# One pool of eight PSUM banks in both mixers, the bank chosen by the step that lets it go

## The chip, the cores and the metric

The kernel runs on one core of a Trainium2 chip. The time is the device time of one execution in microseconds (us), the median of several. The core's engines work beside one another and meet at semaphores: TensorE (PE) multiplies matrices into PSUM, VectorE (DVE) and ScalarE (ACT) read and write PSUM and SBUF, GpSimd (POOL) works on SBUF, SyncE (SP) issues the weight DMAs. PSUM has eight banks of 128 partitions x 512 fp32 values.

## The reference, cut to what matters

A batch of one sequence, 512 tokens of 1024 features, goes through seven parts in a row. The change touches the first and the sixth.

```python
h = x
h = h + mamba2_mixer(rmsnorm(h, ...), ...)                 # first mixer
h = h + swiglu_ffn(rmsnorm(h, ...), ...)                   # ffn 0
h = h + conformer_conv_module(rmsnorm(h, ...), ...)
h = h + swiglu_ffn(rmsnorm(h, ...), ...)                   # ffn 1
x = rmsnorm(h, final_norm)                                 # first block ends
x = x + 0.5 * g1 * swiglu(modulate(rmsnorm_2(x, ...), ...), ...)   # ffn 2
x = x + g2 * (merged @ w_out)     # second mixer: window attention (8 heads, sink) and
                                  # differential attention (4 heads), RoPE, gated and merged
x = x + 0.5 * g3 * swiglu(modulate(rmsnorm_2(x, ...), ...), ...)   # ffn 3
```

The first mixer is a Mamba-2 layer: one projection gives z (16 tiles of 128 features), x (16 tiles), B and C (4 groups each) and the step sizes dt; x, B and C go through a causal convolution of 4 taps and silu; then the state-space scan in 4 chunks of 128 tokens for 32 heads, a norm per group with the gate z, and the output projection.

## The kernel before

Activations lie transposed: h is 8 tiles of 128 features x 512 tokens. A linear layer is a helper (`linear`, L477): for each of its input tiles three matmuls of 128x128 weights on 512 tokens (L486 to L488), since operand and weight are each split in a rounded part (XH, WH) and a rest (XL, WL). Weights come in one long stream of 391 chunks of 8 tiles: SP loads a chunk into `raw`, ACT or POOL rounds it, POOL makes the rest.

Every engine runs its own program, written as a plain sequence. In the mixers all programs go through the same list of steps, `mamba_order()` (L99) and `mixer_order()` (L127), each doing its share of a step. A step of the first mixer is "u", "b", "c" (a tile of x, B, C), "z", "o" (an output tile of the group before), "dec", "A" (the products "cb" of C and B, and B transposed into "Bt"), "B", "C", "D" (transposes "xt" of x, the states "st" in the three banks "S", the first two heads "p"), "E" (two heads' output "Y" and the next two "p"), "H" and "I" (the group's sum of squares "gq" and its spread "qw"). In the second mixer "sA", "vA", "pA" are scores, transposes and products of the window attention, "sB", "tB", "pB" those of the differential one, "k1" to "q2" norm and rotation ("tf", "tw", "rot"), "l" a linear (q, k, v, the gates ga and gb, the branch ba).

Whatever PE makes is a block with a key and needs a PSUM bank. `bank(key, of)` (L456) takes the next one of the tuple `of` in turn and, if an earlier block holds it, waits for the mark ("free", holder), which DVE or ACT sets with the instruction that reads the holder last. A wait stops everything behind it in PE's sequence. `linear` asks for the banks of all its keys before its first matmul. The turn is kept in a dictionary whose key is the tuple itself.

- First mixer: LIN = (0, 1, 2) for linears, TR = (3, 4) for transposes, heads, "cb", "dec", "gq", "qw", SY = (5, 6, 7) for the states and Y; its first linears, eight blocks in all, use ALL (L499).
- Second mixer: MIX = (0, 1, 2, 3, 4), SB = (5, 6) for "sB", OB = (7,) for the window attention's output (L782); its last two loops of linears, "bb" and "wo", use ALL.
- Feed-forward parts: ALL, all eight in turn. Conformer: CB = (0, 1, 2, 3, 4) and XB = (5, 6, 7) (L722); its first linear takes two pairs of banks from CB and XB.

The whole program is built twice: the first pass counts each engine's marks, the second one knows for every key which count of which semaphore it is (`Steps.known`).

Of the kernel before, what the change touches and what calls it, by code (L numbers as in the profile page):

```python
# [175 lines left out]

class Steps:
# [3 lines left out]
    def __init__(self, known=None):  # L181
        self.known, self.made, self.sems = known, {}, {}
# [17 lines left out]
class Counter:  # L200
# [25 lines left out]
def build(nc, dram, steps):  # L226
    at, noted = steps.at, steps.noted
    stream = []
    with ExitStack() as ctx:
# [221 lines left out]
        def pe_program(e):  # L451
            w = Waits(e)
            did = steps.counter("pe")
            turn, holds = {}, {}

            def bank(key, of):  # L456

                n = turn[of] = turn.get(of, -1) + 1
                b = of[n % len(of)]
# [17 lines left out]
            def linear(keys, tiles, slots, ready, of, between=None):  # L477

                bs = [bank(k, o) for k, o in zip(keys, of if isinstance(of[0], tuple) else [of] * len(keys))]
# [17 lines left out]
            ALL, LIN, TR, SY, LO = tuple(range(8)), (0, 1, 2), (3, 4), (5, 6, 7), (0, 1, 2, 3)  # L497
# [38 lines left out]
            def mamba():  # L536
# [7 lines left out]
                def factor(i):  # L544

                    if i == NT - 2:
                        w.wait_ge(s_cst, 16)
                        sum_of("s0", ALL)
                    if i == NT - 1:
                        w.wait_ge(*at("rstd", "s0"))  # L550
                        spread(("s0", "w"), small("s0"), ALL)

                linear([("dt", 0), ("u", 16), ("u", 20), ("u", 0)], [dts, tile(16), tile(20), tile(0)], X8, raw_x, ALL,
                       factor)
                linear([("u", 1)], [tile(1)], X8, raw_x, ALL)
                linear([("u", 2)], [tile(2)], X8, raw_x, ALL)
# [19 lines left out]
                for what, g, i in mamba_order():  # L576
                    par = g % 2
                    if what in ("u", "b", "c"):
                        m = conv_tile((what, g, i))
                        if m not in FIRST:  # L580
                            linear([("u", m)], [tile(m)], X8, raw_x, LIN)
                    elif what == "z":
                        linear([("z", 4 * g + i)], [column("ssm_w_in", 0, 4 * g + i)], X8, raw_x, LIN)
                    elif what == "o":
                        linear([("o", g, i)], [[wt("ssm_w_out", 0, 4 * g + j, i) for j in range(4)]],
                               [8 + 4 * par + j for j in range(4)], lambda j: ("x", "g", 4 * g + j), LIN)
                    elif what == "dec":
                        b = bank(("dec", 0), TR)
# [5 lines left out]
                        b = bank(("dec", 1), TR)  # L594
                        w.wait_ge(*at("dg"))
                        e.matmul(b[:, 0:P], ones, dt_dg, start=True, stop=True).then_inc(*did(("sum", "dec", 1)))
                    elif what == "A":
                        b = bank(("cb", g), TR)
# [6 lines left out]
                        turned(("Bt", g), Bf[par], 3, TR)  # L605
                    elif what in "BCD":
                        if what == "C":
                            S = [bank(("S", g, c), SY) for c in range(3)]
# [3 lines left out]
                        if what in "BC":  # L612
                            for j in ((0, 1) if what == "B" else (2, 3)):
                                w.wait_ge(*at("uv", 4 * g + j))
                                turned(("xt", g, j), xs[par][j], 4, TR)
# [3 lines left out]
                    elif what == "E":  # L619
                        n = 8 * g + 2 * i  # L620
                        Y = bank(("Y", g, i), SY)
# [1590 lines left out]
```

## Time and profile before

| | us |
|---|---|
| median of 3 runs | 2612.82 (2610.52 to 2614.27) |
| the profiled execution | 2610.64 |
| its span, first to last instruction | 2608.8 |
| PE / DVE / POOL / ACT busy | 2516.2 / 1265.1 / 1048.6 / 920.8 |
| mean granted TensorE clock | 0.976 |

The granted clock is 1.00 at 2.4 GHz and 0.5 at 1.2 GHz; a stretch of 0.75 was half the time at either. Durations in a timeline are those of one instruction (or of a merged group, then with its count) on one engine; matmuls overlap, so one of 512 columns has 0.39 us of its own, while 24 in a row take 5.44 us. A bracket behind a row is the time that the engine was idle before it, with the engine and line of the instruction that released it. The line can be a helper's: L1406 is the helper for a scalar-tensor-tensor instruction, L533 that of the transposes, L502 the token sums. In the tiles' names the numbers of buffers are left out: `arena` holds most tiles of the mixers.

### The profile page before, as it was taken

Reading aid. Unit: us, or ns where it says so; the run is one execution under the profiler, and the core shown is the slowest. Engines: PE = TensorE matmul, PEld = TensorE weight load, DVE = VectorE, ACT = ScalarE, POOL = GpSimd, SP = SyncE. Lnnn points to the kernel's source line nnn. Section 1 sums busy time; section 2 is a strip of 40 time slices with the busy share of each in tenths; the row PEclk is TensorE's granted clock in tenths of the full one; section 3 lists DMA queues with packets and bytes.
Section 4 is the critical chain, followed back from the end, with each engine's and each line's share of the span. In section 5 each row is a group of like instructions: output and inputs, shape, how many; then the busy total and the mean of one; then the engine's idle time right before and its main releaser. Section 6 shows DMA issues by size and latency. Waiting matters only on the chain.

```text
span 2608.8 us, 29205 instructions
## 1 busy us (share of the span) xinstructions
PE 2516.2 (96%) x11835; PEld 2054.5 (79%) x11835; DVE 1265.1 (48%) x2010; ACT 920.8 (35%) x1527; POOL 1048.6 (40%) x480
## 2 busy tenths in 40 slices
PE   8989998899999999999999999999999999999999
PEld 6768887788888887788888788887766678788887
DVE  6766666554445697454434632225355545422222
ACT  3424434222223386222223232223455553222221
POOL 4333343544444410654444444443322234544442
PEclk9989999899999998999999999999999999999999
DMA  4112221354442310354432233332211112223222
GB/s 152 49 49 68 70 75 57 126 179 162 161 161 96 98 33 9 129 180 161 162 113 96 90 97 97 97 97 73 73 49 49 49 58 96 81 97 97 97 97 89
DMA packets 70982, 252.56 MB, mean 97 GB/s; under 512 B 8000, under 2 KB 8512, under 8 KB 70848
## 3 DMA queue, kind: packets, MB, share of 16 engines
q1 hardware_dynamic: 58752, 210.27, 25.0%
q10 hardware_dynamic: 12096, 40.42, 4.3%
q8 instruction: 94, 1.54, 0.2%
q14 instruction: 40, 0.33, 0.0%
HBM read 248.56 MB, written 2.10 MB: 96 GB/s over the span
## 4 chain that ended last, share of the span: by engine, by line
PE 85%; DVE 10%; ACT 4%; issue 1%; POOL 0%; ACTq 0%; DMA 0%; DVEq 0%; POOLq 0%
PE ps L486 25%; PE ps L487 25%; PE ps L488 25%; PE ps L502 2%; DVE tmpm L1406 1%; DVE arena L1406 1%; PE ps L526 1%; DVE XL L1415 1%; PE ps L564 1%; PE ps L533 1%; PE ps L717 1%; PE ps L719 1%; PE ps L718 1%; PE ps L632 1%; PE ps L863 1%
## 5 line engine op out<-in xcount | busy, mean ns | idle before, releaser
L2103 POOL TENSOR_TENSOR WL<-raw,WH 128x1024 fp32r<-128x1024 f32 x391 | 951.0, 2434 | 1277.6 <-ACT WH L902 1270.8
L486 PE MATMUL ps<-XH,WH 128*128 128x512 f32 x3160 | 1253.0, 397 | 35.4 <-DVE XL L1406 15.5
L487 PE MATMUL ps<-XL,WH 128*128 128x512 f32 x3160 | 1239.1, 392 | 0.0
L488 PE MATMUL ps<-XH,WL 128*128 128x512 f32 x3160 | 1238.6, 392 | 0.0
L486 PEld LDWEIGHTS ps<-XH,WH 128*128 128x128 f32 x3160 | 600.5, 190 | 170.9 <-issue 22.8
L488 PEld LDWEIGHTS ps<-XH,WL 128*128 128x128 f32 x3160 | 598.8, 190 | 126.6
L487 PEld LDWEIGHTS ps<-XL,WH 128*128 128x128 f32 x3160 | 600.4, 190 | 124.4 <-issue 2.2
L902 ACT ACTIVATE WH<-raw 128x1024 fp32r<-128x1024 f32 x306 | 322.3, 1057 | 738.6 <-PE ps L488 603.6
L1406 DVE SCALAR_TENSOR_TENSOR arena<-arena,ps 128x512 f32<-128x512 f32 x88 | 60.4, 686 | 525.2 <-ACT arena L1098 512.4
L2101 POOL CAST WH<-raw 128x1024 fp32r<-128x1024 f32 x85 | 98.2, 1156 | 261.0 <-PE ps L488 239.2
L1406 DVE SCALAR_TENSOR_TENSOR h<-ps,der,h 128x512 f32<-128x512 f32 x104 | 77.4, 750 | 160.4 <-PE ps L488 160.2
L1456 DVE TENSOR_TENSOR h<-h,ps 128x512 f32<-128x512 f32 x128 | 85.4, 684 | 93.3 <-PE ps L488 92.9
L1102 ACT ACTIVATE XH<-ps 128x512 fp32r<-128x512 f32 x88 | 52.7, 599 | 177.5 <-DVE ps L1720 92.2
L1415 DVE TENSOR_TENSOR XL<-ps,XH 128x512 fp32r<-128x512 f32 x92 | 63.5, 690 | 58.6 <-ACT XH L1102 58.5
L1682 DVE CUSTOM_DVE_ANT_0 arena<-arena 128x1024 f32<-128x1024 f32 x72 | 91.9, 1313 | 0.0
L1098 ACT ACTIVATE arena<-ps 128x512 f32<-128x512 f32 x88 | 51.6, 587 | 65.0 <-DVE ps L1712 49.5
L1406 DVE SCALAR_TENSOR_TENSOR arena<-ps,vec,arena 128x512 f32<-128x512 f32 (+29 forms) x95 | 64.6, 726 | 0.4
L1406 DVE SCALAR_TENSOR_TENSOR tmpm<-ps,der,tmpm 128x509 f32<-128x509 f32 (+2 forms) x72 | 53.9, 749 | 21.4 <-ACT tmpm L979 19.7
L1712 DVE TENSOR_TENSOR ps<-ps,rsm 128x512 f32<-128x512 f32 x44 | 30.5, 694 | 38.6 <-PE ps L488 34.0
L919 ACT ACTIVATE tmpm<-h 128x512 f32<-128x512 f32 x49 | 30.5, 623 | 52.0 <-DVE h L1406 41.6
L1406 DVE SCALAR_TENSOR_TENSOR XL<-h,vec,XH 128x512 fp32r<-128x512 f32 x32 | 36.4, 1138 | 24.2 <-ACT XH L911 24.2
L998 ACT ACTIVATE arena<-ps,arena 128x128 f32<-128x128 f32 x128 | 36.4, 370 | 21.4 <-PE ps L564 21.4
(250 smaller groups left out, 1935.0 us busy)
## 6 DMA issues: line engine op xcount, KB each, us to landing
raw<-in_w SPq DMA_DIRECT2D x394, 512.0 KB, 3.7
arena<-in_w_mod ACTq DMA_DIRECT2D x72, 512.0 KB, 4.4
o_out<-h SPq DMA_DIRECT2D x8, 256.0 KB, 2.0
h<-in_x SPq DMA_DIRECT2D x4, 256.0 KB, 7.2
h<-in_x ACTq DMA_DIRECT2D x4, 256.0 KB, 6.4
raw<-in_w SPq DMA_DIRECT2D x2, 256.0 KB, 4.1
arena<-in_c ACTq DMA_DIRECT2D x1, 512.0 KB, 6.3
vec<-in_vec ACTq DMA_DIRECT2D x1, 295.5 KB, 9.8
```

The lines of the kernel that those rows point to most:

```text
L486: e.matmul(b, wh, XH[:, x, :], start=i == 0, stop=False)
L487: e.matmul(b, wh, XL[:, x, :], start=False, stop=False)
L488: p = e.matmul(b, wl, XH[:, x, :], start=False, stop=i == len(slots) - 1)
L502: p = e.matmul(b[:, c * n:(c + 1) * n], src[:, c * P:(c + 1) * P], mat, start=start and c == 0, stop=stop and c == 3)
L902: A(WH[:, c % NSPL, :], raw[:, c % NRAW, :], ACT.Copy).then_inc(*did(("hi", c)))
L1102: A(XH[:, 8 + 4 * (g % 2) + i, :], ps("up", n, j), ACT.Copy).then_inc(*did(("xhi", "a", n, j)))
L1406: return e.scalar_tensor_tensor(out=out, in0=a, scalar=s, in1=b, op0=op0, op1=op1)
L1415: TT(XL[:, slot, :], src, XH[:, slot, :].bitcast(F32), SUB).then_inc(*did(("x", *key), *free))
L1456: TT(h[:, m, :], h[:, m, :], ps(*key), ADD).then_inc(*marks)
L1682: e.tensor_tensor_reduce(out=t, in0=t, in1=crow, scale=1.0, scalar=0.0, op0=MUL, op1=ADD, accum_out=modv[:, i:i + 1]).then_inc(*did(("mod" ...
L2101: e.tensor_copy(hi, x).then_inc(*did(("hi", c)))
L2103: e.tensor_tensor(lo, x, hi.bitcast(F32), SUB).then_inc(*did(("split", c)))
```

## The change

Both mixers' blocks (all that had ALL, LIN, TR, SY or (5,) in the first, ALL, MIX, SB or OB in the second, up to "bb") take their bank from one pool of eight, named ANY. In the second pass of the build the bank is the one whose holder is let go at the earliest (stage, step), where the stage is the part (0 to 6) and the step the place in the mixer's list at which the engine that sets ("free", holder) does so; a bank without holder, and all that is let go outside a list, counts as (stage, 0) or lower, and ties go by turn. In the first pass the pool goes by turn. ACT's and DVE's programs note stage and step as they go; their instructions, their order and those of PE stay as they are.

```diff
+def placed(stage, order):
+
+    return (((stage, k + 1), step) for k, step in enumerate(order))
...
     def __init__(self, known=None):
-        self.known, self.made, self.sems = known, {}, {}
+        self.known, self.made, self.sems, self.now = known, {}, {}, (0, 0)
...
             self.steps.made[k] = (self.name, self.n)
+            if k[0] == "free":
+                self.steps.note(("let go", *k[1:]), self.steps.now)
...
             turn, holds = {}, {}
+            ANY = None
+
+            def let_go(b):
+
+                n = (b - turn[ANY] - 1) % 8
+                return (*(steps.known["let go", *holds[b]] if b in holds else (0, 0)), n)
 
             def bank(key, of):
 
-                n = turn[of] = turn.get(of, -1) + 1
-                b = of[n % len(of)]
+                if of is ANY and steps.known:
+                    turn.setdefault(of, -1)
+                    b = turn[of] = min(ALL, key=let_go)
+                else:
+                    n = turn[of] = turn.get(of, -1) + 1
+                    b = (of or ALL)[n % len(of or ALL)]
                 if b in holds:
                     w.wait_ge(*at("free", *holds[b]))
...
-            ALL, LIN, TR, SY, LO = tuple(range(8)), (0, 1, 2), (3, 4), (5, 6, 7), (0, 1, 2, 3)
+            ALL = tuple(range(8))
...
-                linear([("u", 3)], [tile(3)], X8, raw_x, (5,))
+                linear([("u", 3)], [tile(3)], X8, raw_x, ANY)
...
-                    b = bank(("p", n), TR)
+                    b = bank(("p", n), ANY)
...
-                            S = [bank(("S", g, c), SY) for c in range(3)]
+                            S = [bank(("S", g, c), ANY) for c in range(3)]
...
-                MIX, SB, OB = (0, 1, 2, 3, 4), (5, 6), (7,)
...
-                            b = bank(("sB", hd, qb, t), SB)
+                            b = bank(("sB", hd, qb, t), ANY)
...
-                for what, g, i in mamba_order():
+                for steps.now, (what, g, i) in placed(0, mamba_order()):
...
-                for what, n, i in mixer_order():
+                for steps.now, (what, n, i) in placed(5, mixer_order()):
...
-            mamba()
-            ffn(0)
-            conformer()
-            ffn(1)
-            ffn(2)
-            mixer()
-            ffn(3)
+            for stage, (does, *n) in enumerate(((mamba,), (ffn, 0), (conformer,), (ffn, 1), (ffn, 2), (mixer,), (ffn, 3))):
+                steps.now = stage, 0
+                does(*n)
```

The last three pieces stand in ACT's and DVE's programs. All other requests of the two mixers change from their tuple to ANY in the same way.

## Rows read from the trace of the kernel before

**Rows 1.** From the page: busy time and share of each engine, and the chain that ended last.

```profile
PE 2516.2 (96%) x11835; PEld 2054.5 (79%) x11835; DVE 1265.1 (48%) x2010; ACT 920.8 (35%) x1527; POOL 1048.6 (40%) x480
...
PE 85%; DVE 10%; ACT 4%; issue 1%; POOL 0%; ACTq 0%; DMA 0%; DVEq 0%; POOLq 0%
```

**Rows 2.** Timeline of PE, first mixer: start, duration, group xcount [idle before <-releaser].

```profile
61.67 2.07 PE L603 MATMUL ps<-arena 128*128 128x128 f32 x8 [4.76 <-DVE arena L1406]
...
83.11 2.93 PE L572 MATMUL ps<-arena 128*128 128x128 f32 x12 [4.60 <-DVE arena L1406]
...
146.91 1.86 PE L502 MATMUL ps<-cst,summ 128*128 128x1 f32 x8 [4.77 <-DVE arena L1613]
...
167.87 1.11 PE L533 MATMUL ps<-cst,arena 128*128 128x128 f32 x4 [4.75 <-DVE arena L1406]
...
245.97 1.05 PE L502 MATMUL ps<-cst,summ 128*128 128x1 f32 x8 [1.97 <-DVE arena L1613]
...
268.43 0.50 PE L486 MATMUL ps<-XH,WH 128*128 128x512 f32 x1 [1.28 <-DVE arena L1406]
...
467.26 0.79 PE L486 MATMUL ps<-XH,WH 128*128 128x512 f32 x1 [2.42 <-DVE h L1456]
...
477.38 0.77 PE L486 MATMUL ps<-XH,WH 128*128 128x512 f32 x1 [5.70 <-DVE h L1456]
```

**Rows 3.** Timeline of PE, second mixer.

```profile
1846.75 0.50 PE L486 MATMUL ps<-XH,WH 128*128 128x512 f32 x1 [0.93 <-ACT tmpm L1292]
...
1875.44 1.12 PE L814 MATMUL ps<-arena 128*128 128x512 f32 x2 [0.82 <-ACT tmpm L1292]
...
1936.28 1.65 PE L825 MATMUL ps<-arena 64*128 64x384 f32 x2 [5.08 <-DVE arena L1995]
...
1999.84 1.01 PE L825 MATMUL ps<-arena 64*128 64x384 f32 x2 [3.15 <-DVE arena L1406]
...
2015.62 0.91 PE L825 MATMUL ps<-arena 64*128 64x384 f32 x2 [1.46 <-DVE arena L1995]
```

**Rows 4.** Table by stretch: length, busy time (xcount) of the five engines, granted clock, DMA share, GB/s.

```profile
40.61:46.05 5.44, 5.44 (x25) 4.51 (x25) 4.49 (x9) 0.60 (x1) 3.44 (x2) 1.00 0.29 93
148.79:156.33 7.54, 7.54 (x26) 6.06 (x27) 0.18 (x1) 0.26 (x1) 0.00 (x0) 0.73 0.00 0
169.00:176.58 7.58, 7.58 (x26) 6.02 (x26) 3.81 (x7) 0.60 (x1) 0.00 (x0) 0.71 0.05 21
347.33:357.54 10.21, 8.26 (x33) 6.82 (x34) 2.08 (x4) 3.59 (x5) 1.85 (x2) 0.83 0.16 52
464.86:484.59 19.73, 11.62 (x37) 9.11 (x38) 10.69 (x12) 7.32 (x10) 4.73 (x3) 0.74 0.42 131
2014.17:2024.22 10.05, 8.60 (x32) 6.46 (x34) 5.61 (x18) 3.40 (x8) 1.30 (x2) 0.83 0.17 53
```

**Rows 5.** Timeline of DVE, first mixer.

```profile
63.77 0.69 DVE L1613 TENSOR_TENSOR arena<-ps,cst 128x512 f32<-128x512 f32 x1 [1.44 <-PE ps L603]
...
82.36 0.69 DVE L1406 SCALAR_TENSOR_TENSOR arena<-ps,tmpm 128x512 f32<-128x512 f32 x1
...
93.42 0.69 DVE L1604 TENSOR_TENSOR arena<-ps,rsm 128x512 f32<-128x512 f32 x1 [4.02 <-PE ps L488]
...
172.99 0.56 DVE L1570 TENSOR_TENSOR arena<-arena 128x384 f32<-128x384 f32 x1
...
184.29 0.69 DVE L1604 TENSOR_TENSOR arena<-ps,rsm 128x512 f32<-128x512 f32 x1 [2.47 <-PE ps L488]
...
469.27 0.68 DVE L1456 TENSOR_TENSOR h<-h,ps 128x512 f32<-128x512 f32 x1
```

**Rows 6.** Timeline of PE, then of DVE, where the conformer part begins.

```profile
843.15 0.39 PE L486 MATMUL ps<-XH,WH 128*128 128x512 f32 x1
...
846.42 0.67 DVE L1456 TENSOR_TENSOR h<-h,ps 128x512 f32<-128x512 f32 x1
```

**Rows 7.** Timeline of DVE, second mixer.

```profile
2014.87 0.69 DVE L1995 TENSOR_TENSOR arena<-ps,arena 128x512 f32<-128x512 f32 x1
```

More of the change, by code:

```diff
@@ L477, in linear @@
             def linear(keys, tiles, slots, ready, of, between=None):
-                bs = [bank(k, o) for k, o in zip(keys, of if isinstance(of[0], tuple) else [of] * len(keys))]
+                bs = [bank(k, o) for k, o in zip(keys, of if isinstance(of, list) else [of] * len(keys))]
                 for i, x in enumerate(slots):
@@ L580, in mamba @@
                         if m not in FIRST:
-                            linear([("u", m)], [tile(m)], X8, raw_x, LIN)
+                            linear([("u", m)], [tile(m)], X8, raw_x, ANY)
                     elif what == "z":
-                        linear([("z", 4 * g + i)], [column("ssm_w_in", 0, 4 * g + i)], X8, raw_x, LIN)
+                        linear([("z", 4 * g + i)], [column("ssm_w_in", 0, 4 * g + i)], X8, raw_x, ANY)
                     elif what == "o":
                         linear([("o", g, i)], [[wt("ssm_w_out", 0, 4 * g + j, i) for j in range(4)]],
-                               [8 + 4 * par + j for j in range(4)], lambda j: ("x", "g", 4 * g + j), LIN)
+                               [8 + 4 * par + j for j in range(4)], lambda j: ("x", "g", 4 * g + j), ANY)
                     elif what == "dec":
-                        b = bank(("dec", 0), TR)
+                        b = bank(("dec", 0), ANY)
                         w.wait_ge(*at("acs"))
@@ L593, in mamba @@
                         p.then_inc(*did(("sum", "dec", 0)))
-                        b = bank(("dec", 1), TR)
+                        b = bank(("dec", 1), ANY)
                         w.wait_ge(*at("dg"))
@@ L781, in mixer @@
             def mixer():
[L782 removed]
                 def x_at(i):
                     return "x", "n1", i
[L787 removed]
+                sum_of("s5", ANY)
                 w.wait_ge(*at("rstd", "s5"))
[L789 removed]
+                spread(("s5", "w"), small("s5"), ANY)
                 w.wait_ge(s_mix, 32)
@@ L800, in mixer @@
                         linear([("ba", i)], [[("w_branch_a_2", 0, ((64 * k, 64), (64 * (k + 4), 64)), ((i * P, P),))
-                                              for k in range(4)]], [8, 9, 10, 11], lambda k: ("x", "oa", k), MIX)
+                                              for k in range(4)]], [8, 9, 10, 11], lambda k: ("x", "oa", k), ANY)
                     elif what == "l":
-                        linear([(n, i)], [tiles(n, i)], X8, x_at, MIX)
+                        linear([(n, i)], [tiles(n, i)], X8, x_at, ANY)
                     elif what in ("k1", "q1"):
-                        b = bank(("tf", n, i), MIX)
+                        b = bank(("tf", n, i), ANY)
                         w.wait_ge(*at("sqr", n, i))
@@ L809, in mixer @@
                         w.wait_ge(*at("rstd", n, i))
-                        spread(("tw", n, i), small(n, i), MIX, 2)
+                        spread(("tw", n, i), small(n, i), ANY, 2)
                     elif what in ("k3", "q2"):
-                        b = bank(("rot", n, i), MIX)
+                        b = bank(("rot", n, i), ANY)
                         w.wait_ge(*at("xs", n, i))
@@ L1590, in squares @@
                         TT(acc0, acc0, tmp[noted("th", "sq", g, j)], ADD).then_inc(*did(("gacc", g, j), ("th_free", "sq", g, j)))
-                for what, g, i in mamba_order():
+                for steps.now, (what, g, i) in placed(0, mamba_order()):
                     par = g % 2
@@ L1997, in rotate @@
                     TT(dst, dst, x, ADD).then_inc(*did(("y", n, i)))
-                for what, n, i in mixer_order():
+                for steps.now, (what, n, i) in placed(5, mixer_order()):
                     if what == "l" and n in ("ga", "gb"):
@@ L2077, in mixer @@
                     sum_squares("s6", m)
-            mamba()
-            ffn(0)
-            conformer()
-            ffn(1)
-            ffn(2)
-            mixer()
-            ffn(3)
+            for stage, (does, *n) in enumerate(((mamba,), (ffn, 0), (conformer,), (ffn, 1), (ffn, 2), (mixer,), (ffn, 3))):
+                steps.now = stage, 0
+                does(*n)
         def pool_program(e):
```

44 lines of the change are left out of this document (21 added, 23 removed).

## Prediction, made before the changed kernel was run

> **What bounds the kernel now.** The reader starts with the page's busy shares and chain: TensorE (PE) is busy 96% of the span and is 85% of the chain that ended last, VectorE (DVE) is 10% and ScalarE (ACT) 4% of it [rows 1]. So only what PE waits for, or what slows its clock, can be won. Next come the timeline's PE rows that carry a bracket, an idle time with its releaser. In the first mixer eight of them stand at a place where the code asks for a PSUM bank, and the releaser is the instruction that empties that bank, not the one that makes the data: 4.76, 4.60, 4.77, 4.75, 1.97, 1.28, 2.42 and 5.70 us [rows 2]; there is one more of 1.97 us, 103 us behind the fifth. In the second mixer there are 0.93, 0.82, 5.08, 3.15 and 1.46 us [rows 3], and the pair of the last two comes once more 69 us later. Together 32 + 16 = 48 us of stop. How one tells a bank stop: at 61.67 PE starts "cb" of group 0, whose inputs B and C were made long before; the releaser is the last step of x tile 0, the holder of bank 3, because TR has two banks only. At 146.91 the sum of squares waits for the multiplication that empties the "cb" bank; at 467.26 and 477.38 an output tile waits for the addition into h.
>
> Behind a stop the clock falls. A linear of 24 matmuls takes 5.44 us at a granted clock of 1.00 (2.4 GHz); the two that follow the stops at 146.91 and 167.87 take 7.54 and 7.58 us at 0.73 and 0.71, thus partly at 1.2 GHz: 2.1 us each on top of the stop [rows 4].
>
> **The change, part by part.** It adds no instruction and no byte to any engine; waits of PE move, and bank numbers change. I worked the new rule through: for each block in PE's order, the holder with the smallest (stage, step) of its "free", ties in turn. Each stop named above gets a bank that, at the old times, was empty before PE asked. But the same DVE and ACT chains make data that PE wants next, so each stop is followed to the next thing that is late.
>
> A, first group, up to z tile 3. The blocks held at the start fill all eight banks, and the earliest holder for the second "dec" block is again x tile 0: about 3 us of stop come back there. DVE runs this part with hardly a pause; what it waits for PE is 1.44 us, for "cb" [rows 5], which goes since "cb" is early. So x tile 3, whose last step ends at 83.05 [rows 5], is ready at 81.6, and PE needs it as data for its transposes: the stop of 4.60 moves there, it doesn't vanish. From there a transposition (0.4) and z tile 3 (5.4) end at 87.5; now DVE gets it at 93.42 [rows 5]. That is 5.9 us at full clock; the new gap of some 4 us will pull the clock down over z tile 3, as it did at [rows 4], 2 us. I take 4; bounds 2 and 6.
>
> B, end of group 0 and start of group 1. The stop of 4.77 goes, with it 2.1 of slow linear [rows 4] and 0.8 of slow small matmuls (8 took 1.86 at 146.91, 1.05 at 245.97 [rows 2]): 7.7, and DVE, which waits for that linear, moves with it. The stop of 4.75 and its 2.1 go too, but PE then meets DVE: it needs the second decayed x tile, finished by DVE at 173.55 [rows 5], with the shift 165.9. Then some 1.6 of small blocks and a linear of 5.44 end at 172.9, against 184.29 now [rows 5]: 11.4. The new gap of 3 to 4 us costs about 2 of clock. I take 9; bounds 7 and 12.
>
> C, group 1 to 2: 1.97 + 1.28 = 3.3 and a little clock; after it DVE waits for PE, so it stays: 3.5 (3 to 4). D, group 2 to 3: the stretch that holds the second stop of 1.97 takes 10.21 us for 33 matmuls at 0.83 [rows 4]; a token sum (0.8) and a linear (5.44) are 6.2: 4.0 (3 to 4).
>
> E, the tail and the start of the first feed-forward part. From output tile 7 to the first chunk of gate and up 19.73 us pass, at 0.74 [rows 4]; the work is 2.72 + 5.44 = 8.2. With eight banks the output tiles never wait, yet the first linear takes four banks at once, and the fourth is that of output tile 5, added into h by 469.95 [rows 5]; 469.95 + 5.44 = 475.4 against 484.6: 9.2. The remaining gap of 2.4 us may cost half a clock drop. I take 8.3; bounds 7 and 9.5. Weights are no bar: GpSimd, which splits them, is busy 40% of the span [rows 1].
>
> F, a place that the text of the change doesn't touch. The conformer takes its pairs of banks from XB = (5, 6, 7), and `turn` is kept by the tuple: SY of the first mixer is the same tuple, and its 28 blocks have moved the turn on by one. Without them XB starts at bank 5. With the turn of ALL as before (8 blocks less are 0 mod 8), bank 5 is held by the last "down" tile of the part before. PE starts that linear at 843.15, as the one before it runs out, and DVE empties the bank at 847.09 [rows 6]. The linear takes its four banks before its first matmul, so PE's whole queue stands for 3.7 us; with 1.7 for a clock drop a loss of 5.4; bounds 3.7 and 6.2 (the clock costs nothing, or 2.5). Nothing else in the fixed pools comes close.
>
> G, second mixer. The stops of 0.93 and 0.82 go, DVE and ACT wait for PE there: 1.9 with clock. In the three long ones DVE is behind and PE only walks into it a few blocks on. In the third: at 2015.56 DVE empties the bank of "rot" [rows 7], PE starts at 2015.62 [rows 3]; under the new rule the linear two blocks later gets the same bank, so it can't start before 2015.6. Now it ends at 2024.2, in a stretch at 0.83 [rows 4]; then 2015.6 + 5.5 = 2021.1: 3.1 is left of the two stops' 4.6 and their clock. The repeat gives 3.1 too. The stop of 5.08 returns as some 2 us at the second score block (the bank emptied at 1936.28 [rows 3] again) and as more at the last transposition of the head, whose input DVE makes: some 1.6 left. Sum 9.7, I take 9; bounds 4 (the lead is eaten by DVE) and 16 (DVE and ACT gain from being served earlier: half of the stops' 14 us and of their slow clock more).
>
> Sum: 4 + 9 + 3.5 + 4 + 8.3 - 5.4 + 9 = 32.4 us. The profiled execution took 2610.6 us (span 2608.8), so 2578.2; it lay 2.2 under the median of 2612.8, which gives 2580. Bounds: 2 + 7 + 3 + 3 + 7 - 6.2 + 4 = 20 and 6 + 12 + 4 + 4 + 9.5 - 3.7 + 16 = 48, thus 2565 to 2593.
>
> **Rivals.** (1) DVE and ACT set the pace in both mixers, and stops only change place. For: they share the work that PE waits for, at all but two stops the releaser is DVE. Against: DVE itself waits for the linears of PE at 93.42 (4.02 us) and 184.29 (2.47 us) [rows 5]. Left are C, D, 7 of E, 1.9 of G less 6.2 for F: 10, so 2603. (2) Half clock at every gap. Some dozen shorter gaps stay (two in A, one in B, one in E, one in F, seven or so in G). If each costs some 2.5 of clock, as the old ones did (D: 10.21 - 1.97 - 6.2 = 2.0; E: 19.73 - 8.2 - 2.42 - 5.70 = 3.4 for two), where I counted it at five of them, 7 x 2.5 = 18 come on top: a gain of 14, 2598. For: the slow linears of [rows 4]; against: the first matmul after the stop of 1.28 took 0.50 us, those after 2.42 and 5.70 took 0.79 and 0.77 [rows 2], so a short stop need not slow the clock. The Trainium skill, "TensorE: Matmul & The Clock Gate", section "A second HAM failure mode: psum-queue depth-cycling", has this rule against cycling through banks: brief idles between groups of matmuls make the clock swing, and throughput suffers; by that rule the time would be this 2598. No row shows such a swing without a stop of over a microsecond. (3) PE's lead pays in full: 48 us of stops and about 27 of slow clock, less 5.4: 70, so 2543; against it stand the data waits of A, B and G. (4) Slower: stops break into pieces, each with its clock drop, where linears run densely. Place: the second mixer and the conformer's start; price: 2.5 a drop. It decides once more than 32.4 / 2.5 = 13 drops come on top of those counted; 2620 at 16 of them. Against: each old stop of over 4 us has such a drop already. (5) The rule falls back to a plain rotation of eight, because a "free" has no step: every holder gets one in the first pass of the build, so hardly; then about 2590.
>
> **How the numbers follow.** Chances: forecast 0.68, (1) 0.12, (2) 0.12, (3) 0.04, (4) 0.03, (5) 0.01. The range takes the forecast's 2565 to 2593 and (2), to 2598 above, and one us more below. 0.2% (5 us), about what a measurement of this kernel can tell from no change, is missed only by the upper end of (1) and by (4): faster 0.94, same 0.03, slower 0.03.
>
> **What would show it.** Right: no PE bracket at the "cb", "S", "gq", "xt" and output blocks; z tile 3 reaches DVE about 4 us earlier, the last output tile of group 3 runs without a stop, the first feed-forward part starts 25 to 30 us earlier; a new PE bracket of 3 to 4 us, released by DVE's addition into h, at the first linear of the conformer; in the second mixer brackets of 2 to 3 us at "tB", "sB" and "ga". Wrong: the first mixer's gain under 20 us (then DVE's chain was shorter of slack than I read), the clock share there no better than 0.95, or no stop in the conformer (then my turn count is off).

## The result, and the profile after

The changed kernel takes 2585.71 us (median of 4 runs, 2584.54 to 2588.12), the kernel before 2611.67 beside it: a ratio of 0.990, 95% interval 0.988 to 0.992, so 26 us are gained where 32 were forecast. The profiled execution took 2588.12 us with a span of 2586.3, at a granted clock of 0.980 (before 0.976).

From the page of the changed kernel, the lines that answer to [rows 1]. Columns: busy time, share of the span and instructions of each engine, then the chain that ended last.

```profile
PE 2507.2 (97%) x11835; PEld 2049.5 (79%) x11835; DVE 1278.4 (49%) x2010; ACT 920.0 (36%) x1527; POOL 1044.4 (40%) x480
...
PE 85%; DVE 10%; ACT 3%; issue 1%; POOL 0%; ACTq 0%; DMA 0%; DVEq 0%; POOLq 0%
```

The instruction counts are the same. Of the 22.5 us by which the span is shorter, PE is busy for 9.0 less (the same matmuls with less time at half clock) and idle for 13.5 less. DVE is 13 us **more** busy with the same 2010 instructions, so some of them take longer now. This is spread over the whole kernel and is 6 us in a second profile; where the forecast went wrong, in the first mixer's tail, it is 0.7 us. The busy time doesn't show that error: what matters there is which instruction is slow, and when.

The timeline of PE, first mixer, changed kernel (start, duration, group xcount [idle before <-releaser]); the line numbers of PE's first mixer have grown by 17 and those of DVE's instructions named here by 11, so L550 is the transpositions, L589 the states, L503 a linear's first matmul, L1417 the scalar-tensor-tensor helper.

```profile
62.31 0.79 PE L613 MATMUL ps<-arena,cst 128*128 128x128 f32 x2 [3.20 <-DVE arena L1417]
...
82.21 1.12 PE L550 MATMUL ps<-cst,arena 128*128 128x128 f32 x4 [2.87 <-DVE arena L1417]
...
161.83 2.90 PE L589 MATMUL ps<-arena 128*128 128x128 f32 x12 [4.16 <-DVE arena L1581]
...
456.48 0.77 PE L503 MATMUL ps<-XH,WH 128*128 128x512 f32 x1 [5.35 <-DVE h L1467]
```

The stops for "cb" and "gq" of [rows 2] are gone: 4.76, 4.77, twice 1.97, and with them 1.28 before a z tile and 2.42 before an output tile. What is left are data waits (82.21: transposing x tile 3; 161.83: decayed x tiles of group 1, released by L1581) and two waits for a bank: 3.20 at the second "dec" block, as forecast, and 5.35 at ffn 0's first linear, forecast as 2.4.

Then PE where the conformer begins, and in the second mixer, changed kernel:

```profile
825.19 0.47 PE L503 MATMUL ps<-XH,WH 128*128 128x512 f32 x1 [3.84 <-DVE h L1467]
...
1913.65 0.66 PE L550 MATMUL ps<-cst,arena 128*128 128x128 f32 x4 [1.52 <-DVE arena L1417]
1917.20 2.07 PE L868 MATMUL ps<-arena 64*128 64x512 f32 x2 [1.55 <-DVE arena L2006]
...
1979.73 0.44 PE L550 MATMUL ps<-cst,arena 128*128 128x128 f32 x2 [1.43 <-DVE arena L1417]
1992.61 0.66 PE L550 MATMUL ps<-cst,arena 128*128 128x128 f32 x4 [1.43 <-DVE arena L1417]
1996.16 0.79 PE L503 MATMUL ps<-XH,WH 128*128 128x512 f32 x1 [2.90 <-DVE arena L2006]
```

The stop of 3.84 is the one forecast for a place that the change doesn't name. The 5.08, 3.15 and 1.46 of [rows 3] have become 1.52 and 1.55, 1.43 and 1.43, and 2.90.

How far the kernel is ahead of the one before can be read wherever PE ends a given block. In the table a term is what is gained between two such blocks; each profile is one execution, so the changed kernel was profiled a second time (e10_again, below). A counts from the start of the span, and the start isn't part of the change: at the end of x tile 1, before any stop, the first profile was 0.6 us behind the kernel before and the second 1.0 ahead. Without this A is 4.2 and 3.1.

| term | forecast | first profile | second profile |
|---|---|---|---|
| A to z tile 3 | 4 | 3.5 | 4.1 |
| B to z tile 6 | 9 | 8.3 | 10.2 |
| C to z tile 8 | 3.5 | 3.8 | 3.8 |
| D to x tile 14 | 4 | 3.8 | 3.8 |
| E to gate tile 2 of ffn 0 | 8.3 | 2.4 | 2.7 |
| F first linear of the conformer | -5.4 | -5.7 | -5.7 |
| from there to the second mixer | 0 | 1.5 | 0.1 |
| G second mixer | 9 | 4.8 | 6.1 |
| sum | 32.4 | 22.5 | 25.1 |

A to D and F came out within 1.2 us of the forecast. E and G are the miss.

### The profile page after: what moved, and what is told of

The parts are those of the page before. It is cut to its first block, busy times and chain, and to the rows that moved or that the text cites. A ratio compares the mean times of both kernels' runs of the same rounds, so it can differ in the third digit from the quotient of the medians.

```text
span 2586.3 us, 29205 instructions
## 1 busy us (share of the span) xinstructions
PE 2507.2 (97%) x11835; PEld 2049.5 (79%) x11835; DVE 1278.4 (49%) x2010; ACT 920.0 (36%) x1527; POOL 1044.4 (40%) x480
## 4 chain that ended last, share of the span: by engine, by line
PE 85%; DVE 10%; ACT 3%; issue 1%; POOL 0%; ACTq 0%; DMA 0%; DVEq 0%; POOLq 0%
PE ps L503 25%; PE ps L504 25%; PE ps L505 25%; PE ps L519 2%; DVE arena L1417 1%; PE ps L543 1%; PE ps L581 1%; DVE XL L1426 1%; PE ps L734 1%; DVE tmpm L1417 1%; PE ps L735 1%; PE ps L736 1%; PE ps L649 1%; PE ps L550 1%; DVE XL L1417 1%
## 5 line engine op out<-in xcount | busy, mean ns | idle before, releaser
L503 PE MATMUL ps<-XH,WH 128*128 128x512 f32 x3160 | 1252.8, 396 | 40.8 <-DVE XL L1417 16.0
L503 PEld LDWEIGHTS ps<-XH,WH 128*128 128x128 f32 x3160 | 600.5, 190 | 176.1 <-issue 22.6
L1417 DVE SCALAR_TENSOR_TENSOR arena<-arena,ps 128x512 f32<-128x512 f32 x88 | 60.4, 686 | 513.7 <-ACT arena L1113 503.2
L1417 DVE SCALAR_TENSOR_TENSOR h<-ps,der,h 128x512 f32<-128x512 f32 x104 | 77.4, 750 | 160.4 <-PE ps L505 160.2
L1417 DVE SCALAR_TENSOR_TENSOR arena<-ps,vec,arena 128x512 f32<-128x512 f32 (+29 forms) x95 | 64.7, 728 | 0.4
L1417 DVE SCALAR_TENSOR_TENSOR tmpm<-ps,der,tmpm 128x509 f32<-128x509 f32 (+2 forms) x72 | 53.9, 749 | 21.4 <-ACT tmpm L994 19.7
L1723 DVE TENSOR_TENSOR ps<-ps,rsm 128x512 f32<-128x512 f32 x44 | 30.5, 694 | 37.7 <-PE ps L505 34.0
L1417 DVE SCALAR_TENSOR_TENSOR XL<-h,vec,XH 128x512 fp32r<-128x512 f32 x32 | 37.1, 1158 | 24.5 <-ACT XH L926 24.5
L934 ACT ACTIVATE tmpm<-h 128x512 f32<-128x512 f32 x49 | 30.5, 622 | 52.0 <-DVE h L1417 41.6
L1440 DVE TENSOR_TENSOR summ<-summ,tmpm 128x512 f32<-128x512 f32 x36 | 42.7, 1187 | 8.4 <-ACT tmpm L934 8.4
## 6 DMA issues: line engine op xcount, KB each, us to landing
vec<-in_vec ACTq DMA_DIRECT2D x1, 295.5 KB, 10.2
```

The lines of the kernel that those rows point to most:

```text
L503: e.matmul(b, wh, XH[:, x, :], start=i == 0, stop=False)
L1417: return e.scalar_tensor_tensor(out=out, in0=a, scalar=s, in1=b, op0=op0, op1=op1)
```

## Experiments

**Each mixer alone.** In e1_first_only all blocks of the second mixer, in e2_second_only all of the first have their old sets back; one line of each:

```diff
-linear([(n, i)], [tiles(n, i)], X8, x_at, ANY)
+linear([(n, i)], [tiles(n, i)], X8, x_at, MIX)
-linear([("u", m)], [tile(m)], X8, raw_x, ANY)
+linear([("u", m)], [tile(m)], X8, raw_x, LIN)
```

> The pool of eight in the first mixer alone; the second mixer has its three sets MIX, SB, OB as before. Theory (gains add up part by part: first mixer about +22 to PE's mark at ffn 0's first linear, the conformer's first linear gives 5.8 back, and the second mixer holds 4.4 of the changed kernel's 26): about 21 us faster than before, 2590, with PE's stop of 3.8 us at the conformer's first linear and, in the second mixer, the stops of the kernel before (5.1 and 3.2 us released by DVE). Rival (the second mixer runs as it does because it starts 18 us earlier, its banks are worth nothing): within 1 us of the changed kernel's 2586.

> The pool of eight in the second mixer alone; the first mixer has ALL, LIN, TR and SY as before. Theory: the banks of the second mixer are worth 4 to 5 us, so 4.5 us faster than before, 2607, and no stop at the conformer's first linear, since the turn of ALL is as before. Rival A (my forecast's sizes for the second mixer were right and something in the first mixer's new timing ate half of them): 9 us faster, 2603. Rival B (they are worth nothing): within 1 us of before.

e1: 2593.18, a ratio to before of 0.993 (0.9915 to 0.9945), 19 us gained. e2: 2605.74, 0.9976 (0.9966 to 0.9986), 6.3 gained. 19 + 6.3 = 25 of the 26: the halves add up, and both rivals that let one half feed on the other fall. The second mixer is worth 6 to 7 us, more than the 4.8 of the first profile and less than the forecast's 9.

**The stop at the conformer, twice.** XB starts one bank further; e14_xb_again is the same kernel on another chip.

```diff
-CB, XB = (0, 1, 2, 3, 4), (5, 6, 7)
+CB, XB = (0, 1, 2, 3, 4), (6, 7, 5)
```

> The changed kernel, but XB, the three banks for the conformer's conv tiles, starts one bank further: (6, 7, 5) in place of (5, 6, 7). Theory (the stop of 3.84 us at the conformer's first linear comes from the turn of ALL alone, which the first mixer's eleven blocks no longer push on: its block meets the bank of ffn 0's last output tile, and half clock behind the stop makes it 5.8): the stop goes, about 5.8 us faster than the changed kernel, 2580. Rival A (the stop only uncovers a wait for DVE's data of the same chain): the stop stays at 3 us or more and the gain is under 1 us. Rival B (only the wait goes, the clock was no part of it): about 3.8 us faster, 2582.

> The changed kernel with XB = (6, 7, 5) once more, nothing else. The first time the conformer's start was 5.7 us shorter and the whole kernel only 2.7. Theory (1.6 us pieces of half clock fell at three places behind it by chance of that profile): the conformer's start is again 5.7 shorter, the stretch from conv tile 8 to 12 takes 32.7 or 34.3, and the median of more runs is 3.5 to 6 us under the changed kernel's 2585.8. Rival (a stop at the conformer's start shifts what follows so that it runs with less half clock, and half of the price is given back for good): the median stays 2583 within 0.8.

e3: 2583.05, 0.9889 (0.9872 to 0.9905). e14: 2582.22, 0.9889 (0.9873 to 0.9906). In both the bracket of 3.84 is gone, and the way from ffn 0's gate tile 10 to the conformer's first conv tile takes 231.88 us, as before the change, in place of 237.61: the mechanism and its local price of 5.7 stand. But the whole kernel gained only 0.0012 x 2612 = 3 us. The intervals of the two ratios overlap that of the changed kernel, yet all eight times with the turned XB (2580.8 to 2584.0) lie below all eight of the changed kernel (2584.5 to 2588.1). Where the rest went, PE in windows of e14, then of the changed kernel, from the first conv tile's end (columns: length, PE busy (xcount), granted clock, DMA share, GB/s):

```profile
839.84:847.00 7.16, 6.59 (x38) 0.87 0.23 73
847.00:874.14 27.14, 27.14 (x118) 0.97 0.23 78
```

```profile
846.82:854.00 7.18, 6.61 (x42) 1.00 0.23 73
854.00:879.50 25.50, 25.50 (x114) 1.00 0.26 83
```

The same blocks, 34.30 us against 32.68: 1.6 of half clock more, in e3 as in e14, and in no other kernel. Another 0.7 to 1.6 lie between ffn 1's gate tile 9 and ffn 2's first (277.49 us in both, 275.91 and 276.76 in the two profiles of the changed kernel). e14's median of 2582.22 lies inside both forecasts, so it decides nothing by itself. The rival says that half of the price is given back because the stop is gone. The next experiment removes the same stop and leaves XB as it is: the way to the first conv tile is again 231.88 us, and the stretch behind it, e4_ffn0b in the same view, has no half clock:

```profile
835.61:868.28 32.67, 32.10 (x155) 1.00 0.25 81
```

The same 32.7 us stand in e9, e11, e12 and e13, in e2 and in the kernel before, all without this stop, and the last two have the same conformer banks as e3. So the missing stop alone does not give the 1.6 us back, nor do those banks: the rival's mechanism is not shown. Why the clock falls there in e3 and e14, without a stop of its own, stays open. The reason that e3's expectation gives, eleven blocks of the first mixer that no longer push the turn of ALL, is wrong: the code takes eight there, and eight change nothing in a turn of eight. It is the turn of XB, as the prediction has it.

**The turn of banks in ffn 0.** All of ffn 0 takes FB in place of ALL, and ahead of the conformer the turn of ALL is set.

```diff
+FB = (6, 7, 0, 1, 2, 3, 4, 5) if n == 0 else ALL
...
+turn[ALL] = 93
```

> The changed kernel, but ffn 0 takes its banks in the turn 6, 7, 0 to 5 instead of 0 to 7, so that the four banks of its first linear are those of the output tiles 0 to 3 of the first mixer, which DVE has added into h long before; the turn of ALL is then set so that the later parts have the banks of the changed kernel. The conformer's conv tile meets another bank too, so its stop goes as well. Theory (in the tail of the first mixer PE isn't stopped by a lack of banks of its own but by which bank ffn 0's first linear is given: a stop of 5.35 us that costs about 2 more in half clock): both stops go, about 13 us faster than the changed kernel, 2573; 7 of them are this tail's, seen against the run with XB alone changed. Rival (the first linear needs x, and x needs DVE's chain, which is as late as the bank: the stop is renamed, not removed): the stop at the first linear stays at 4 us or more, now for data, and the gain is that of XB alone, 2580.

2578.93, 0.9874 (0.986 to 0.9889): 6.8 us faster than the changed kernel, not 13. PE at the norms of ffn 0 and of the conformer, the only stops of over half a microsecond at the two places, e4_ffn0b:

```profile
475.13 2.08 PE L543 MATMUL ps<-cst,smallm 128*128 128x128 f32 x8 [3.98 <-DVE smallm L1455]
...
840.28 1.16 PE L543 MATMUL ps<-cst,smallm 128*128 128x128 f32 x8 [0.57 <-DVE smallm L1455]
```

The stop of 5.35 is gone, but PE stops for 3.98 at 471 us, 23 us after the last output tile, at the small matmul that spreads ffn 0's norm factor: the factor needs the sum of squares of all eight output tiles, and DVE is late with it. The gate and up tiles needed the bank, their norm needs DVE's chain. From x tile 14 to gate tile 2 it is 149.5 us in place of 151.5: 2 us of the 7 expected. By subtraction the other 4.8 of the 6.8 us are the conformer's stop, whose local price is 5.7. The rival, "renamed, not removed", was nearer, though at another instruction.

**What makes DVE late in the tail.** DVE, then POOL, changed kernel:

```profile
438.94 0.68 DVE L1440 TENSOR_TENSOR summ<-summ,tmpm 128x512 f32<-128x512 f32 x1
...
441.90 2.88 DVE L1440 TENSOR_TENSOR summ<-summ,tmpm 128x512 f32<-128x512 f32 x1
...
447.34 2.87 DVE L1440 TENSOR_TENSOR summ<-summ,tmpm 128x512 f32<-128x512 f32 x1
...
452.78 2.82 DVE L1440 TENSOR_TENSOR summ<-summ,tmpm 128x512 f32<-128x512 f32 x1
455.52 0.68 DVE L1467 TENSOR_TENSOR h<-h,ps 128x512 f32<-128x512 f32 x1
```

```profile
441.51 2.71 POOL L2110 TENSOR_TENSOR WL<-raw,WH 128x1024 fp32r<-128x1024 f32 x1
...
446.95 2.71 POOL L2110 TENSOR_TENSOR WL<-raw,WH 128x1024 fp32r<-128x1024 f32 x1
...
452.39 2.66 POOL L2110 TENSOR_TENSOR WL<-raw,WH 128x1024 fp32r<-128x1024 f32 x1
```

The same instruction takes 0.68 us alone and 2.8 to 2.9 where POOL's rest pass lies over it; DVE's ends 0.55 us after POOL's each time. The experiment leaves the rest pass out:

```diff
+if 57 <= c <= 60:
+    ...
+    e.tensor_copy(hi, x).then_inc(*did(("hi", c), ("split", c)))
+    continue
```

> The changed kernel, but POOL leaves out the rest (WL) of weight chunks 57 to 60, which are read by ffn 0's first linears; they take stale rests, so the output is another, and PE's instructions are the same. Theory (in the first mixer's tail DVE's XL and L1440 instructions take 2.7 to 2.9 us instead of 0.7 to 1.1 because POOL's rest pass of 2.7 us reads SBUF at the same time; four such meetings make the add of o,3,5 late and PE's stop long): those DVE instructions take 1.1 us or less, the stop of 5.35 us at ffn 0's first linear shrinks to under 1 us, and by PE's mark at gate tile 2 the kernel is 5 to 7 us earlier than the changed one; about 6 faster in all, 2580. Rival (DVE's own work in the tail is what is late, POOL's pass only falls beside it): the stop stays at 4 us or more and the gain is under 1 us.

2579.7, 0.9873 (0.9855 to 0.989), 6.1 us faster than the changed kernel. DVE by groups in its tail, 430 to 452 us (columns: xcount | busy us, mean ns | idle before, releaser), then PE:

```profile
L1467 DVE TENSOR_TENSOR h<-h,ps 128x512 f32<-128x512 f32 x8 | 5.5, 682 | 2.6 <-PE ps L505 2.6
L1417 DVE SCALAR_TENSOR_TENSOR XL<-h,vec,XH 128x512 fp32r<-128x512 f32 x7 | 5.3, 752 | 5.5 <-ACT XH L926 5.5
L1440 DVE TENSOR_TENSOR summ<-summ,tmpm 128x512 f32<-128x512 f32 x6 | 4.1, 684 | 0.0
```

```profile
428.81 0.50 PE L503 MATMUL ps<-XH,WH 128*128 128x512 f32 x1 [1.80 <-DVE XL L1426]
474.54 1.16 PE L543 MATMUL ps<-cst,smallm 128*128 128x128 f32 x8 [0.64 <-DVE smallm L1453]
```

Against the changed kernel's tail, by the same view of 430.7 to 456.4 us:

```profile
L1440 DVE TENSOR_TENSOR summ<-summ,tmpm 128x512 f32<-128x512 f32 x4 | 9.2, 2312 | 0.0
L1417 DVE SCALAR_TENSOR_TENSOR XL<-h,vec,XH 128x512 fp32r<-128x512 f32 x5 | 6.9, 1381 | 4.0 <-ACT XH L926 4.0
L1467 DVE TENSOR_TENSOR h<-h,ps 128x512 f32<-128x512 f32 x6 | 4.1, 679 | 2.6 <-PE ps L505 2.6
```

Between the two PE rows no stop is left, neither the changed kernel's 5.35 nor e4's 3.98, and from x tile 14 to gate tile 2 it takes 143.9 us in place of 151.5. In the end 6.1 of these 7.6 us are gained. The addition h<-h,ps, which reads PSUM and SBUF, is 0.68 in both; only instructions with two inputs in SBUF grow. The Trainium skill, "SBUF — State Buffer", section "Who interferes with whom", says that a DVE instruction with two SBUF inputs contends with a GpSimd instruction that reads SBUF, for a shared pair of ports that one of them holds alone. These traces agree: 684 ns on average without the rest pass; of the four behind the average of 2312, three lay beside it (2.8 to 2.9 us) and one, at 438.94, did not (0.68).

**DVE in the second mixer.** Of each rotation of a k or q tile DVE makes the middle instruction only.

```diff
+if n in "qk":
+    w.wait_ge(*at("sum", "rot", n, i))
+    TT(dst, ps("rot", n, i), sin, MUL).then_inc(*did(("free", "rot", n, i), ("y", n, i)))
+    return
```

> The changed kernel, but in the second mixer DVE leaves out the first and the last of the three instructions of each rotation of a k or q tile (8 tiles, 16 instructions of 0.69 us; the output is another). Theory (in the second mixer's heads DVE, not the banks, sets the pace now: PE waits 2.9 us for L2006 ahead of the linears ga 6 and gb 1, where DVE has queued a rotation just before): these two stops fall to 1.5 us or less, the half clock behind them goes too, and the second mixer is 4 to 8 us shorter than in the changed kernel, about 2580. Rival (the stop ahead of ga 6 is one link of a chain over ACT and PE, DVE's load is not its length): the stops stay at 2.5 us or more and the gain is under 2 us, 2584 or more.

2577.89, 0.9869 (0.9853 to 0.9884), 8 us faster than the changed kernel for 16 x 0.69 = 11 us less of DVE. Of PE's brackets, the one of 2.90 before ga 6 is gone, and so is its repeat (e8_short_rot):

```profile
1988.85 0.65 PE L550 MATMUL ps<-cst,arena 128*128 128x128 f32 x4 [1.43 <-DVE arena L1417]
1997.06 0.55 PE L550 MATMUL ps<-cst,arena 128*128 128x128 f32 x3 [0.59 <-DVE arena L2055]
```

The second mixer is 7.9 us shorter than in the changed kernel's first profile and 7.3 than in its second, though a new stop of 3.19 us for DVE (L1417) appears at 1923.94. With eight banks the heads of the second mixer go at DVE's pace.

**Order in group 1.** On top of e4_ffn0b, z tile 2 ahead of step C; e11 then also starts the pool's turn two banks on.

```diff
+mid = (("z", g, 2), ("C", g, 0)) if g == 1 else (("C", g, 0), ("z", g, 2))
-    turn.setdefault(of, -1)
+    turn.setdefault(of, 1)          # e11 only
```

> The kernel with ffn 0's banks turned (2579), and in group 1 of the first mixer the step z tile 2 stands ahead of step C instead of behind it, on all engines. Theory (the stop of 4.16 us in C is for DVE's transposes of group 1, L1581, and 5.44 us of matmuls moved ahead of it cover it): the stop goes or falls to under 1.5 us, and the kernel is 3 to 5 us faster, about 2575; best of all kernels run. Rival (DVE is the late one there, and z's own DVE step now stands ahead of C's, so the stop only moves): a stop of 3 us or more remains in C or D of group 1, and the time is 2577 to 2581.

> The kernel with z tile 2 ahead of step C in group 1 (2579), but the pool's turn starts two banks further, so that the output tiles of group 3 lie in banks 6, 7, 0 to 5 again and ffn 0's first four banks are those of output tiles 0 to 3. Theory (moving z shifted the pool's choice by two banks and so brought back the stop of 5.32 us at ffn 0's first linear, which ate the 3.1 us gained by then): the stop goes, the norm's small matmul waits some 4 us instead, 2 to 3 us faster than the same without the shift, 2576 to 2577, the fastest of all. Rival (DVE's chain to the norm is the limit either way): 2578.5 to 2580.

e9: 2579.22, no gain on e4's 2578.93, although the stop of 4.16 fell to 2.19 and PE was 2.2 us earlier at z tile 8 and 3.1 at the last output tile. PE, e9_z_ahead, then e11_z_ahead_banks:

```profile
449.91 0.76 PE L504 MATMUL ps<-XH,WH 128*128 128x512 f32 x1 [5.32 <-DVE h L1470]
```

```profile
166.61 0.94 PE L590 MATMUL ps<-arena 128*128 128x128 f32 x6 [2.20 <-DVE arena L1584]
...
471.20 2.07 PE L544 MATMUL ps<-cst,smallm 128*128 128x128 f32 x8 [3.71 <-DVE smallm L1456]
```

Moving one step changed which banks the rule picks, by two, and the stop of 5.3 us, removed by naming banks, was back. With the turn put right, e11 takes 2573.73, 0.9858 (0.9843 to 0.9872): 37 us under the kernel before and the fastest of all. For e9 the rival's time held, but not its mechanism: it wanted a stop of 3 us or more in C or D, where 2.19 was left, and the theory wanted under 1.5. For e11 the theory held, with more than its 2 to 3 us: by the ratios it is 0.0015 x 2612 = 4 us faster than e9.

**Is it the joining or the rule?** Both from the kernel before, first mixer only (the lines are shortened, they also set ALL and LO):

```diff
-LIN, TR, SY = (0, 1, 2), (3, 4), (5, 6, 7)
+LIN, TR, SY = (0, 1), (2, 3, 4), (5, 6, 7)      # e12
+LIN, SY = (0, 1, 2, 3, 4), (5, 6, 7)            # e13: TR's blocks take LIN
```

> The kernel before, with one bank moved in the first mixer: LIN = (0, 1) and TR = (2, 3, 4) in place of (0, 1, 2) and (3, 4). Theory (TR's two banks are what PE stops for in the first mixer, at cb, at xt, at gq twice a group; a linear fills a bank in 5.44 us and its reader is done within that time, so two banks carry most linears): the stops of 4.76 and 4.77 us shrink by 3 us or more each and new ones come where a tile's three taps keep its bank longer than 5.44 us; 5 to 12 us faster than before, 2600 to 2607. Rival (the linears need their third bank as much): as many us of new stops at linears as are saved, within 3 us of before or slower.

> The kernel before, with LIN and TR of the first mixer joined to one set of five banks, (0, 1, 2, 3, 4), in plain turn; SY stays (5, 6, 7), and the second mixer is as before. Theory (it needs the rule that picks the bank let go first: a plain turn meets the slow holders, x tiles and cb, at fixed places): less than half of the 19 us that the pool of eight brings in the first mixer, 0 to 9 us faster than before. Rival (what counts is that the sets are joined, the rule adds little): 12 to 20 us faster than before, 2592 to 2600.

e12 takes 2643.6, 1.0128 (1.0113 to 1.0143): 33 us slower. What PE waits for from 180 to 420 us in e12, then before (columns: total us, times, longest):

```profile
PE ps L486 <- DVE arena L1406: 35.0, 14, 6.7
```

```profile
PE ps L486 <- DVE arena L1406: 1.3, 1, 1.3
```

Up to z tile 6 e12 is 11.6 us ahead of before, as the pool is; then 14 linears stop for a bank. The theory had the first part right; the rival is right for the whole and far too small. e13 takes 2602.09, 0.9968 (0.9955 to 0.9981). By the last output tile it is 19.1 us ahead of before (452.55 against 471.69), the pool 20.5 in its first profile, 23.1 in its second, and 20.5 to 24.0 in all eight profiles that have it there: **a plain turn over LIN and TR together brings most of it in the first mixer; the rule, with SY joined too, adds 1 to 5 us.** There my theory, less than half, fell. For the whole kernel its range of 0 to 9 us held and the rival's 12 to 20 did not, but not for the theory's reason. The kernel keeps 9 of the 19, for two stops of the same sort as F (PE, e13_lintr):

```profile
463.18 0.76 PE L486 MATMUL ps<-XH,WH 128*128 128x512 f32 x1 [10.65 <-DVE h L1456]
...
1062.12 0.79 PE L486 MATMUL ps<-XH,WH 128*128 128x512 f32 x1 [5.32 <-DVE h L1406]
```

At 463.18 one of the first linear's four banks is that of output tile 7, which DVE adds at 462.40; at 1062.12 the conformer's CB, now the same tuple as LIN, ends its turn one bank off, and ffn 1 meets its last tiles. A plain rotation of all eight wasn't tried, so what the rule alone is worth is not shown.

**The same kernel again.**

> The changed kernel once more, nothing altered, for a second profile of the same program. Theory (what half clock costs behind a stop isn't fixed by the kernel: runs of the same instructions have differed by 1.6 us in single stretches): the same stops to 0.1 us, the same time within 2 us, but at least one of the stretches from z tile 3 to u tile 6 (47.55), from p2 tile 7 to gate tile 2 of ffn 1 (30.63) and from gate tile 9 of ffn 1 to gate tile 0 of ffn 2 (275.91) comes out 0.8 or 1.6 us longer or shorter. Rival (the clock follows the instructions alone): every one of these stretches within 0.3 us of the first profile.

2585.82, 0.99 (0.9884 to 0.9916). Most stops of over a microsecond are the same to 0.1 us, but not all: the 2.87 at x tile 3 is 3.70, the 2.90 before ga 6 is 2.53, the 1.55 is 1.84. The stretches differ too: 45.99 us in place of 47.55, 32.10 in place of 30.63, 276.76 in place of 275.91. The rival fell, and so did the theory's "same stops to 0.1 us". PE behind the stop of 2.15 at 128 us, first profile, then second:

```profile
128.41:132.50 4.09, 4.09 (x33) 0.67 0.27 59
132.50:137.41 4.91, 4.91 (x22) 0.93 0.15 61
```

```profile
127.83:132.00 4.17, 4.17 (x39) 1.00 0.28 69
132.00:135.27 3.27, 3.27 (x17) 1.00 0.19 78
```

The same 2.15 us of stop was followed by a clock of 0.67 once and by 1.00 the other time: 9.00 against 7.44 us.

## Why the prediction was right and wrong

The time lies in the range, 5.7 us above the forecast of 2580; the gain of 26 us lies between the lower bound of 20 and the forecast of 32. Of the signs that were named, z tile 3 came 3.5 us earlier, the bracket at the conformer came, the gain at ffn 0's gate tile 2 was 22.0 and 24.6 us, over the 20 that were named, and the clock of the first 430 us was 0.97 (before 0.96). The first feed-forward part started 20.9 and 23.5 us earlier, not 25 to 30.

**A to D, right.** z tile 3 reached DVE at 89.89 in place of 93.42 [rows 5]; the stop of 4.60 moved to the transposition of x tile 3 (2.87) and 3.2 us of it to "dec", both named beforehand. In B the forecast had PE meet DVE at the decayed x tile: the bracket of 4.16 is that. C and D were the sum of their stops and clock, as read from [rows 2, 4]. That B came out 2 us apart in the two profiles is chiefly the clock behind the stop of 2.15 us.

**E, the step that failed: "against 484.6: 9.2" with DVE's addition of output tile 5 at the old 469.95 [rows 5].** I set the stop to 2.4 by moving PE's tail up against a DVE that I took to be no slower than before. But before, PE's stop of 2.42 [rows 2] held up POOL too. POOL, kernel before:

```profile
452.49 2.40 POOL L2103 TENSOR_TENSOR WL<-raw,WH 128x1024 fp32r<-128x1024 f32 x1
...
457.93 2.72 POOL L2103 TENSOR_TENSOR WL<-raw,WH 128x1024 fp32r<-128x1024 f32 x1
462.25 1.04 POOL L2101 CAST WH<-raw 128x1024 fp32r<-128x1024 f32 x1 [1.60 <-PE ps L488]
463.38 2.69 POOL L2103 TENSOR_TENSOR WL<-raw,WH 128x1024 fp32r<-128x1024 f32 x1
471.81 1.18 POOL L2101 CAST WH<-raw 128x1024 fp32r<-128x1024 f32 x1 [5.75 <-PE ps L488]
```

Up to the addition of output tile 5 DVE met three rest passes, those of 452.49, 457.93 and 463.38. After 466 POOL waits for PE to use up a chunk, and DVE's additions of output tiles 5 and 6 pass undisturbed. Without the stop POOL keeps its cadence of 5.44 us and meets DVE once more ahead of the addition of output tile 5: four passes, from that of 436.07 on. The addition came at 456.2; PE was then 5.35 us late in place of 2.4. Term: 8.3 forecast, 2.4 and 2.7 measured; e7 shows that 7.6 us more are there once POOL is out of the way, e4 that banks alone give 2. Of the 5.9 us between the forecast and the first profile this longer stop is 3.0. The other 3.1 the changed kernel can't be blamed for: the profile of before had luck in this stretch. From output tile 3 of group 2 to output tile 1 of group 3 it took 28.8 us; all thirteen other profiles took 30.5 to 31.9 for the same instructions. With the first mixer's old banks and the same stops, e2_second_only took 157.2 us from x tile 14 to gate tile 2, before took 154.0. PE in before, then in e2, over the same two blocks of small matmuls and linear:

```profile
442.62:451.25 8.63, 6.31 (x25) 1.00 0.19 63
```

```profile
443.66:453.89 10.23, 7.89 (x25) 0.83 0.16 52
```

Against e2's tail the pool wins 157.2 - 151.5 = 5.7, against before's 2.4. So E lies between 2.4 and 5.7, and 8.3 was too much by either. No run shows what a second execution of the kernel before takes here.

**F, right as a mechanism and at its place:** 3.84 us of bracket for 3.7 (the rows give 847.09 - 843.15 = 3.9), 5.7 of loss for 5.4; DVE lets the bank go at 825.1 and PE starts at 825.19, in the order that [rows 6] let expect. Removing the stop gave 3 us at the kernel's end in e3 and e14, where half clock came behind it, and 4.8 in e4, where none did.

**G, the term mis-sized: 9 forecast, 4.8 and 6.1 measured, 6.3 by e2's median.** By the second profile the first two stops gave 2.1 (forecast 1.9), the three heads 0.6, 1.1 and 1.0 (forecast 1.6, 3.1, 3.1), and the end 1.3 (forecast 0). The failing line is "then 2015.6 + 5.5 = 2021.1": the bank came when I said, but the linear behind it ran at half clock for a part. PE from the stop of 2.90 to the end of ga 6, changed kernel:

```profile
1996.16:2003.83 7.67, 7.67 (x26) 0.73 0.16 59
```

7.67 in place of 5.5: 2.2 us a head, just what is missing in two of them. I had counted no clock there though [rows 4] show 0.83 for the same stretch before. That DVE is behind in these heads, as forecast, is what e8 shows.

**Rivals.** (1), DVE sets the pace: true for the heads of the second mixer (e8) and the tail (e7), not for A to D. (2), half clock at every gap, 2598: behind the gap of 1.43 us at 1979.73 the clock stayed at 1.00 for the next 10 us; behind the pair of 1.52 and 1.55 it was 0.52, PE, changed kernel:

```profile
1914.60:1921.50 6.90, 5.35 (x10) 0.52 0.24 76
```

Behind 2.87 at 82.21 four transpositions took 1.12 us in place of 0.44, and behind 2.90 the linear was slow. The Trainium skill's rule on the swinging clock, "TensorE: Matmul & The Clock Gate", section "A second HAM failure mode: psum-queue depth-cycling", would have given that 2598, and the measured 2585.7 does not bear it out. Of the 18 us on top of the forecast that this needs the traces show 4.4 at the two stops of 2.90 and about 2.7 at the pair (5.35 us of matmuls at half clock); over the whole kernel PE spent 9.0 us less on slow clock than before, not more. (1) gave 2603, (3) and (4) are off by 43 and 34 us. (5), at 2590, is nearest in number, but its mechanism isn't there: worked through by the code, the rule takes another bank than the next in turn for some thirty of the first mixer's 164 blocks, and moving one step in e9 shifted its choice by two banks, which a plain rotation could not do. That a plain rotation might cost little more is what e13 suggests for two of the three sets.

## What to carry to other kernels

PSUM banks split by purpose make PE wait for one slow holder while other banks stand empty; join the sets first, and look at the rule that picks among them last. How the eight banks are split is delicate: one bank moved from the linears to the transposes cost 33 us in e12. A bank stop that goes is replaced by the next late thing: follow the reader's chain with its neighbours at their **new** times, since an engine that no longer stops may meet another's slow passes once more. Where parts of a kernel meet, check by name which holder the next part's first blocks get, after every change of order: here such meetings cost 2 to 6 us each.

## What the runs showed of the hardware

- A DVE instruction of 128x512 with two inputs in SBUF takes 0.68 us alone and 2.8 to 2.9 beside POOL's tensor_tensor on 128x1024; one that reads PSUM and SBUF stays at 0.68. POOL's own pass takes 2.7 us then and 2.4 alone.
- A stop's price in clock isn't fixed: the same stop of 2.15 us cost 1.6 us in one execution and nothing in another. Three stretches of the same kernel differed by 0.9 to 1.6 us between its two profiles, and one of the kernel before by 1.7 to 3.1 from all others, so a single profile measures a term of this sum to about 1.6 us, and in one case to 3.
- One such piece came twice with one kernel: 34.3 in place of 32.7 us from conv tile 8 to 12 in both profiles with the turned XB, in none of the other twelve; the cause is open.
